# Mixer attention: two head pairs' scores and weighted sums at once, in rotating PSUM banks, and key sums in two matmuls

## The reference, cut to what matters

```python
h = xn @ w_in                     # q, k, v, and b_c, c_c, h_c, two gates
y_conv = b_c * causal_dwconv(c_c * h_c, conv_w_mix)
branch_conv = y_conv @ w_proj_conv
z = einsum("bqhd,bkhd->bhqk", q, k) * scale          # 16 heads of 64
log_beta = log_sigmoid(z)
log_fail = where(causal, log_beta - z, 0)
survive = cumsum(log_fail, axis=keys, reverse=True) - log_fail
a = where(causal, exp(log_beta + survive), 0)
o = einsum("bhqk,bkhd->bqhd", a, v)
branch_attn = o @ w_proj_attn
merged = sigmoid(g_conv + b0) * branch_conv + sigmoid(g_attn + b1) * branch_attn
out = merged @ w_out
```

## Time and profile before

| | |
|---|---|
| median of 3 runs | 835.04 us (835.02 to 835.27) |
| profiled execution, its own time | 835.41 us |
| its span, first to last instruction | 833.4 us |
| PE busy | 823.3 us, 99% of the span |
| DVE busy | 618.3 us, 74% |
| ACT busy | 503.9 us, 60% |
| POOL busy | 127.6 us, 15% |
| the loop over p, from the first scores to the last | 63.7 to 168.8 us |

### The profile page before, as it was taken

The page is one execution under the profiler, slowest core; times in us unless marked ns, Lnnn a source line. Parts: engine busy times, 40 slices in busy tenths (PEclk is TensorE's granted clock), DMA queues, the critical chain, the costliest instruction groups (busy, mean ns, idle before and its releaser), DMA issues.

```text
span 833.4 us, 16961 instructions
## 1 busy us (share of the span) xinstructions
PE 823.3 (99%) x6832; PEld 798.2 (96%) x6832; DVE 618.3 (74%) x1029; ACT 503.9 (60%) x875; POOL 127.6 (15%) x120
## 2 busy tenths in 40 slices
PE   9999999999999999999999999999999999999997
PEld 8999999999999999999999999999998999889896
DVE  6657888877666689767664478998888696568755
ACT  7446666555444576555554368787968554356655
POOL 1000000000000305443441100043515010000002
PEclk9999999999999999999999999999999999999999
DMA  8754434345656536656666525646545376554331
GB/s 317 262 165 140 142 112 167 127 153 180 189 189 180 180 105 197 201 181 185 191 196 188 189 91 168 196 140 192 176 140 174 109 229 183 190 170 136 127 101 51
DMA packets 39853, 139.81 MB, mean 168 GB/s; under 512 B 4432, under 2 KB 5088, under 8 KB 39648
## 3 DMA queue, kind: packets, MB, share of 16 engines
q1 hardware_dynamic: 38160, 135.90, 51.1%
q10 hardware_dynamic: 1616, 2.84, 1.1%
HBM read 137.65 MB, written 1.06 MB: 166 GB/s over the span
## 4 chain that ended last, share of the span: by engine, by line
PE 88%; DVE 7%; ACT 2%; POOL 1%; issue 1%; DMA 1%; SPq 0%; DVEq 0%; ACTq 0%; POOLq 0%
PE ps L1852 66%; PE ps L1917 4%; PE ps L1876 4%; PE ps L1855 4%; DVE weights_lo L1111 2%; PE ps L2037 1%; PE ps L2063 1%; PE ps L2325 1%; PE ps L2344 1%; PE ps L1973 1%; PE ps L1879 1%; PE ps L2333 1%; PE ps L2048 1%; ACT weights_hi L566 1%; DVE arena L1422 1%
## 5 line engine op out<-in xcount | busy, mean ns | idle before, releaser
L1111 DVE TENSOR_TENSOR weights_lo<-raw_weights,weights_hi 128x1024 fp32r<-128x1024 f32 x251 | 313.9, 1255 | 84.5 <-ACT weights_hi L566 83.4
L566 ACT ACTIVATE weights_hi<-raw_weights 128x1024 fp32r<-128x1024 f32 x250 | 262.2, 1053 | 144.1 <-issue 63.5
L1852 PE MATMUL ps<-x_hi,weights_hi 128*128 128x256 f32 (+3 forms) x1184 | 340.4, 288 | 0.3 <-DVE weights_lo L1111 0.2
L1852 PE MATMUL ps<-x_lo,weights_hi 128*128 128x256 f32 (+3 forms) x1184 | 334.1, 282 | 0.0
L1852 PE MATMUL ps<-x_hi,weights_lo 128*128 128x256 f32 (+3 forms) x1184 | 333.3, 282 | 0.0
L1852 PEld LDWEIGHTS ps<-x_hi,weights_hi 128*128 128x128 f32 x1184 | 223.0, 188 | 4.5 <-issue 3.5
L1852 PEld LDWEIGHTS ps<-x_lo,weights_hi 128*128 128x128 f32 x1184 | 222.9, 188 | 0.7 <-issue 0.5
L1852 PEld LDWEIGHTS ps<-x_hi,weights_lo 128*128 128x128 f32 x1184 | 223.5, 189 | 0.0
L1852 PE MATMUL ps<-y_lo,weights_hi 128*128 128x256 f32 (+1 forms) x488 | 137.5, 282 | 0.0
L1852 PE MATMUL ps<-y_hi,weights_hi 128*128 128x256 f32 (+1 forms) x488 | 137.3, 281 | 0.0
L1852 PE MATMUL ps<-y_hi,weights_lo 128*128 128x256 f32 (+1 forms) x488 | 137.2, 281 | 0.0
(11 more groups left out here) (288 smaller groups left out, 1180.9 us busy)
## 6 DMA issues: line engine op xcount, KB each, us to landing
raw_weights<-weights_in SPq DMA_DIRECT2D x251, 512.0 KB, 3.9
arena<-decay_rows ACTq DMA_DIRECT2D x8, 256.0 KB, 3.8
masks<-masks_in SPq DMA_DIRECT2D x1, 1186.0 KB, 7.7
raw_weights<-weights_in SPq DMA_DIRECT2D x4, 256.0 KB, 4.7
hidden<-xT_in SPq DMA_DIRECT2D x3, 272.0 KB, 5.2
hidden<-xT_in SPq DMA_DIRECT2D x1, 276.0 KB, 3.1
gate_w<-gate_w_in ACTq DMA_DIRECT2D x1, 256.0 KB, 3.7
out<-arena ACTq DMA_DIRECT2D x1, 256.0 KB, 2.1
```

The source lines that it names most:

```text
L566: a.sig(A(whi[:, s * CW:(s + 1) * CW], raw[:, (c % RAW) * CW:(c % RAW + 1) * CW], ACT.Copy), "hi_ready")
L1111: d.sig(TT(wlo[:, s * CW:(s + 1) * CW], raw[:, (c % RAW) * CW:(c % RAW + 1) * CW], whi[:, s * CW:(s + 1) * CW].bitcast(F32), ALU.subtract) ...
L1852: ins = mm(bank(BANK_OF[no])[:, 0:b - a], wt, x_[:, kt, a:b], start=s0, stop=s1)
```

## The change

Five things are changed together.

1. Scores are computed for two pairs at once, at odd p: `scores(p-1)` and `scores(p)` after c(p), and after them `attend(p-3)` and `attend(p-2)`. After the loop come `attend(6)` and `attend(7)` together. The scores of even pairs are in banks 4 and 5, of odd pairs in 6 and 7. The fail terms and weights have four buffers in place of two.
2. The attention outputs of pairs 0 to 5 get two of the banks 0 to 3, inserted in the rotation ahead of h(3), h(5) and h(7). `ATT_EARLIER` is what `attend` waits for; `AFTER_ATT` is the projection that comes next in that bank, which waits for `att_split`. The rotation gives q(4), c(4), q(6), c(6), gc(0) and ga(0) for these.
3. Key sums take two matmuls of 434 and 160 columns for each head and part: GpSimd copies the 16 late query columns behind the others (`q_tail`), so that the scores of one piece have 160 columns in place of 144.
4. The order on PE at even p is q(p), `survive(p-2)`, c(p), `survive(p-1)`, h(p), b(p). On ACT and DVE `fail`, `fail_high`, `fail_low`, `log_weight`, `weights_of`, `att_high` and `att_low` are moved accordingly.
5. The inserted banks shift the rotation of all later projections by two. mk and mv change banks, mq(0) does not: the last output in its bank 0 was the second one of mv(0) before, and is the second one of mv(1) now.

```diff
@@ banks
+        if _s == "h" and _i % 2 and _i > 2:
+            for _p in (_i - 3, _i - 2):
+                ATT_BANK[_p] = (_at + len(ATT_EARLIER)) % 4
+                ATT_EARLIER[_p] = max(m for m in range(_at) if BANK_OF[m] == ATT_BANK[_p])
+            _b = (_at + len(ATT_EARLIER)) % 4
         EARLIER.append(max((m for m in range(_at) if BANK_OF[m] == _b), default=None))
+        for _p in ATT_EARLIER:
+            if ATT_BANK[_p] == _b and ATT_EARLIER[_p] == EARLIER[-1]:
+                AFTER_ATT[_at] = _p
@@ GpSimd
+            for p in range(KT):
+                pool.wait_ge(S("out_taken"), taken[FIRST_OUT["q", p]][1])
+                q = qpair[:, p % 2, :]
+                g.sig(nc.gpsimd.tensor_copy(q[:, T:T + TAIL], q[:, 256:T]), "q_tail")
@@ ScalarE, loop over p
+                if p % 2:
+                    feed(("c", p))
+                    softplus_part(p - 1)
+                    feed(("h", p))
+                    fail_high(p - 1)
+                    if p > 1:
+                        att_high(p - 3)
+                        att_high(p - 2)
+                    softplus_part(p)
@@ VectorE, loop over p
                 if p:
-                    log_weight(p - 1)
+                    if p % 2 == 0:
+                        fail(p - 1)
                     feed(("b", p - 1))
                 feed(("q", p))
+                if p and p % 2 == 0:
+                    log_weight(p - 2)
+                    fail_low(p - 1)
                 r = result(("c", p), 0, T - TC)
...
-                fail(p)
+                if p % 2:
+                    fail(p - 1)
+                elif p:
+                    log_weight(p - 1)
                 r = result(("h", p), 0, T - TC)
...
-                fail_low(p)
+                if p % 2:
+                    fail_low(p - 1)
...
-                if p:
-                    att_low(p - 1)
+                if p % 2 and p > 1:
+                    att_low(p - 3)
+                    att_low(p - 2)
@@ TensorE
             def bank_free(n):
-                if EARLIER[n] is not None:
+                if n in AFTER_ATT:
+                    pe.wait_ge(S("att_split"), AFTER_ATT[n] + 1)
+                elif EARLIER[n] is not None:
                     pe.wait_ge(S(taken[EARLIER[n]][0]), taken[EARLIER[n]][1])
...
-                        mm(zb[:, FG:ZC], at_or_later, f_[:, FG + TAIL:FC], start=False, stop=False,
-                           skip_group_check=True)
-                        mm(zb[:, 0:FG], at_or_later, f_[:, 0:FG], start=False, stop=False, skip_group_check=True)
-                        ins = mm(zb[:, FG:ZE], later, f_[:, 0:FG + TAIL], start=False, stop=n == 1,
+                        mm(zb[:, 0:ZC], at_or_later, f_, start=False, stop=False, skip_group_check=True)
+                        ins = mm(zb[:, FG + TAIL:ZE], later, f_[:, 0:FG + TAIL], start=False, stop=n == 1,
                                  skip_group_check=True)
...
-                if p:
+                if p and p % 2 == 0:
+                    survive(p - 2)
+                project(("c", p), xhi, xlo, TC, T)
+                if p % 2:
...
+                    scores(p - 1)
+                    scores(p)
+                    if p > 1:
+                        attend(p - 3)
+                        attend(p - 2)
+                elif p:
                     survive(p - 1)
```

More of the change, by code:

```diff
@@ L657, in softplus_part @@
                 for e in range(2):
-                    a.step(A(sp[:, e, :], bank(4 + e)[:, 0:ZC], ACT.Abs))
+                    a.step(A(sp[:, e, :], bank(4 + 2 * (p % 2) + e)[:, 0:ZC], ACT.Abs))
                 for e in range(2):
@@ L722, in out_squares @@
                 act.wait_ge(S("out_ready"), FIRST_OUT[stage, KT - 1] + 1)
-                last, h = bank(FIRST_OUT[stage, KT - 1] % 4), (T - t0) // 2
+                last, h = bank(BANK_OF[FIRST_OUT[stage, KT - 1]]), (T - t0) // 2
                 a.sig(A(sq[:, KT - 1, t0:t0 + h], last[:, 0:h], ACT.Square), "sq_half")
@@ L1254, in _ @@
                 d.sig(TT(bb[:, p % 2, :], bb[:, p % 2, :], c_, ALU.mult), "conv_y")
-                if p:
-                    att_low(p - 1)
+                if p % 2 and p > 1:
+                    att_low(p - 3)
+                    att_low(p - 2)
+            fail(KT - 1)
             feed(("b", KT - 1))
             conv_low(KT - 1)
+            fail_low(KT - 1)
             def gate_raw(s, i, j):
@@ L1274, in _ @@
             gate_raw("gc", 0, 0)
-            log_weight(KT - 1)
+            log_weight(KT - 2)
             for i in range(0, KT, 2):
@@ L1280, in _ @@
                     gate_raw("ga", j, 1)
+                    if j == 0:
+                        log_weight(KT - 1)
                     conv_branch(j)
                     if j == 0:
+                        att_low(KT - 2)
                         att_low(KT - 1)
@@ L2036, in scores @@
                         rows = slice(64 * e, 64 * e + 64)
[L2037 removed]
+                        ins = mm(bank(4 + 2 * (p % 2) + e)[:, c0:c0 + t1 - t0], keysT[rows, p, P * k:P * k + P],
                                  qpair[rows, p % 2, t0:t1], start=n == 0, stop=n == 3, skip_group_check=True)
@@ L2057, in attend @@
                 pe.wait_ge(S("a_ready"), 2 * p + 2)
-                need(pe, "att_split", p - 1)
-                for n, (c0, k, t0, t1) in enumerate(PIECES):
+                if p in ATT_EARLIER:
+                    pe.wait_ge(S(taken[ATT_EARLIER[p]][0]), taken[ATT_EARLIER[p]][1])
+                for n, (c0, k, t0, t1) in enumerate(SUMS):
                     for e in range(2):
@@ L2062, in attend @@
                         h = 2 * p + e
-                        ins = mm(bank(6 + p % 2)[rows, t0 - TA:t1 - TA], vals[:, k, 64 * h:64 * h + 64],
-                                 aw[:, e, c0:c0 + t1 - t0], start=n == 0, stop=n == 3, skip_group_check=True)
+                        ins = mm(bank(ATT_BANK[p])[rows, t0 - TA:t1 - TA], vals[:, k, 64 * h:64 * h + 64],
+                                 aw[:, 2 * (p % 2) + e, c0:c0 + t1 - t0], start=n == 0, stop=n == 3, skip_group_check=True)
                 ins.then_inc(S("av_ready"), 1)
-            Q_TAKEN = [taken[FIRST_OUT["q", p]][1] for p in range(KT)]
             pe.wait_ge(S("zeroed"), 3)
@@ L2088, in _ @@
             project(("gc", 0), xhi, xlo, TA, T)
+            survive(KT - 2)
+            project(("ga", 0), xhi, xlo, TA, T)
             survive(KT - 1)
-            project(("ga", 0), xhi, xlo, TA, T)
             conv_projection(0)
+            attend(KT - 2)
             attend(KT - 1)
```

103 lines of the change are left out of this document (56 added, 47 removed).

## The result

The changed kernel takes 861.43 us (median of 5 runs, 860.76 to 864.71) beside 835.27 us for the kernel before (5 runs, 835.02 to 836.99): a ratio of 1.0318, 95% interval 1.0308 to 1.0329. It is 3.2% slower. The forecast was 857.8 us with a range of 850 to 864. Direction, place and range are right. The size is 3.6 us short: the time lies outside the narrower range of 854 to 861 that the forecast gave itself, and within 1 us of the prices of its rivals C (862) and D (861).

What follows compares the result with a forecast made beforehand. PE's stream, busy 99%, sets the time. On 835.4 us: - 1.5 - 1.0 + 13.1 + 7.7 + 0.9 + 1.0 + 1.0 + 1.6 = + 22.8, 858.2; the median lies 0.4 lower, so 857.8 us, range 850 to 864.

Steps and rivals of the forecast that it cites:

- Rival C: Clock falls in every stall ahead of q(4), q(6), gc(0): three half-clock stretches, some lengthened projections; 862 us; chance 16%.
- D: Merged blocks don't save: each second block of scores pays its entry again, stalls at upper bounds; 861 us; chance 4%.
- Gain 1: Scores and weighted sums on PE: fewer changes of array shape, 17.4 us to 15.6; gain 1.5 us (0.5 to 2.2).
- Gain 2: Key sums on PE: two matmuls cost 0.31 us where three cost 0.34; gain 1.0 us (0 to 1.3).
- Loss 1: q(4), q(6) and gc(0) wait for att_split, late in DVE's queue: 4.4 us each, 13.1 us (11.7 to 14.2).
- Loss 2: Second key sums of even turns wait for fail_low: 3.3 us in turn 2, 2.2 twice; 7.7 us (6 to 9).
- Rival B: Bank stalls only: DVE catches up, fail_low on time in turns 4 and 6; 851.1 us; chance 10%.
- Loss 3: Small waits: attend(7) 0.9 us, mq(0)'s bank 1.0, ten weight loads of first matmuls behind waits 1.0.
- Loss 4: PE's clock falls to 1.2 GHz behind 4.4 us stalls: 1.5 us each, one of three taken; 1.6 us (0 to 4.7).
- Rival A: Faster: att_split comes in time, key sums don't wait, only the gains stay; 832.5 us; chance 3%.

Runs made afterwards that it cites:

- the last run: Changed kernel with DVE and ACT queues, mq(0)'s bank and the tail reordered, plus failure logs and log_weight(7) moved against the last waits: 832.23 us, ratio 0.9962.

## Why the prediction was right, and where it was off

**Gain 1, changes of shape: right.** The block of turn 3 and the last sums, the latter where they don't wait (the last run):

```profile
107.32 0.28 PE L1902 MATMUL ps<-x_hi,weights_lo 128*128 128x260 f32 x1
107.53 2.10 PE L2087 MATMUL ps<-arena 64*128 64x160 f32 x32
109.56 1.78 PE L2112 MATMUL ps<-arena 128*64 128x144 f32 x32
111.27 0.39 PE L1902 MATMUL ps<-x_hi,weights_hi 128*128 128x260 f32 x1
111.50 0.28 PE L1902 MATMUL ps<-x_lo,weights_hi 128*128 128x260 f32 x1
```

```profile
185.02 0.28 PE L1901 MATMUL ps<-x_hi,weights_lo 128*128 128x258 f32 x1
185.23 1.82 PE L2111 MATMUL ps<-arena 128*64 128x144 f32 x32
...
187.20 0.28 PE L1901 MATMUL ps<-x_lo,weights_hi 128*128 128x258 f32 x1
```

Measured as the prediction measured: 111.50 - 107.32 - 0.24 = 3.94 (3.85 expected), and 187.20 - 185.02 - 0.24 = 1.94 (1.91). With 2.23 in turn 1, all blocks come to 2.23 + 3 x 3.94 + 1.94 = 16.0 beside 17.4: 1.4 us, 1.5 predicted. So the rival that the new shape of the blocks costs by itself (D in the prediction) falls.

**Gain 2, key sums: 1.3 us, 1.0 predicted.** The pair costs 1.20, not 1.24. The two pieces were off in opposite directions: from start to start the matmuls of 434 columns take 0.23 to 0.24 us, where the line between two rows gave 0.20, and those of 160 columns 0.07 to 0.08, where 0.11 was left. Their sum of 0.31 came out as worked out by luck, and the first of the four sums takes only 0.27. The formula of the Trainium skill (TensorE: Matmul & The Clock Gate, Back-to-back issue gap), by which the gain was 1.6, is as far off on the other side.

**Loss 1, the bank stalls: right in place, cause and size.** From h(3)'s end, 114.13 + 0.28 = 114.41, to the end of the first `att_low`, 121.00 + 0.42 = 121.42, are 7.0 us, as predicted; three stalls of 4.38, 13.1 us.

**Loss 2, the second key sums: 8.6 us, 7.7 predicted.** `survive(1)` takes 94.44 - 90.25 = 4.19 us and starts 0.63 late, beside 127.18 - 125.99 = 1.19 for `survive(2)`, which doesn't wait: 3.6. `survive(3)` takes 133.78 - 130.08 = 3.70, so 2.5 more, and (5) the same. For turn 2 the prediction says that DVE is 1 us late there, while the times it gives say 105.22 - 103.67 = 1.55; with these its 3.3 would have been 3.8, beside the measured 3.6. The rest of the difference is the weight loads, which stood in loss 3. Rival B, in which these waits vanish, falls.

**Loss 3, small ones.** mq(0) waits 1.45 - 0.23 = 1.2 us (762.35 to 763.80 on PE's timeline; 1.1 predicted with its load), attend(7) 0.3 (0.9 predicted).

**Loss 4, the clock: the mis-sized term, 1.6 us predicted, 6.0 measured.** I priced a stretch at 1.5 us and that is what one cost, which is partly luck, since the price was an estimate from the start of the trace. The number of them was wrong: I took one of three stalls, and all three had one, with a fourth behind the stall in turn 2, which I had not counted as able to call one. Rival C named the first half of this, at 16%, and its 862 is nearer to the measured time than the forecast. It deserved more than the forecast's own count, since the one row I had the earlier trace rows spoke for it and none against. The rule of the Trainium skill cited there (TensorE: Matmul & The Clock Gate, What's actually happening), by which an idle array goes to the lower level, agrees in kind with the four stretches. Three of them, though, began only when PE was back at work: q(4) starts at 121.48 and the clock falls at 121.9. The Trainium skill (TensorE: Matmul & The Clock Gate, HAM oscillation — how this bites in real kernels) describes a stream that flips between the levels as its gaps recur; here, with three stalls filled, the next ones called the stretches instead.

**The sum**: - 1.4 - 1.3 + 13.1 + 8.6 + 1.2 + 0.3 + 6.0 = 26.5 beside 26.2 in the spans. The start of the traces, which the change leaves alone, is 0.4 us shorter in the changed kernel's (its 301st matmul stands at 42.64 us, that of before at 43.08), and with that 26.1 is left: the account closes to 0.1 us. The forecast's 22.8 had the clock 4.4 us too low; its other errors are 1 us each at most, some up and some down (the second key sums 0.9 too low; attend(7) 0.6 too high; the weight loads, a term of 1.0, already inside the other terms here), and come to 0.7 too high together. That the size is no further off owes something to this.

Rival A, that only the gains stay, was 832.5 us. (Its limit of 2.9 us from h(3)'s end is 2.7 by its own rows, 100.64 - 97.94; nothing hangs on it.) It is wrong for the change as made, and it is what the last run measures (832.2), once every result that PE waits for has been moved ahead of work that nobody waits for.

## What to carry to other kernels

When an engine at 99% gets its work regrouped, ask for every result that it waits for at which place of the other engine's queue it is made. Here DVE, at 87% of a turn, made results in time for the old order of PE and late for the new one, with the same instructions. Price the stalls as one account: moving one kind of result alone brought a quarter of the loss back (the attention outputs) or made it larger (the failure logs), and all together brought back everything. To the stalls add the clock. In these traces 20 of the 24 waits in which PE was idle for 2.0 us or more had a half-clock stretch, at 1.5 to 3.0 us each.
